# Hybrid decoder layer on eight cores: the first stages by token blocks, the first projection's 2048 columns resident, and the group map folded into the up projection

## What is computed

```python
hn = rmsnorm(x, g_mix)
z = hn @ w_in                      # 1024 -> 4096 columns: u | b | c | h (512 each) | gp | gc (1024 each)
# pooling branch: trailing windows 2/4/8/16 over four channel groups of 128
d = windowed_mean(u) - u
mixed = einsum('btgc,gcd->btgd', d, w_group) * scale
# conv branch: three taps, depthwise, causal
y = sum(w_conv[k] * shift(c * h, 2 - k) for k in range(3)); conv_out = b * y
merged = sigmoid(gp) * (mixed @ w_pool_up) + sigmoid(gc) * (conv_out @ w_conv_out)
x = x + merged @ w_o
# then a SwiGLU FFN (2816), and a gated per-layer embedding, with a final rmsnorm
```

## Time and profile before

| | |
|---|---|
| Runs | 1023.15 us median of 3 (1022.27 to 1025.79) |
| Profiled execution | 1024.13 us, of which the slowest core's span is 1022.5 us (cores 1016.4 to 1022.5) |
| PE busy | 964.5 us, 94% of the span |
| DVE, ACT, POOL busy | 483.6, 258.3, 319.6 us |
| Mean granted TensorE clock of that core | 0.976 |
| DMA | 63.18 MB written, mean 62 GB/s |

### The profile page before, as it was taken

The page is one execution under the profiler, slowest core; times in us unless marked ns, Lnnn a source line. Parts: engine busy times, 40 slices in busy tenths (PEclk is TensorE's granted clock), DMA queues, the critical chain, the costliest instruction groups (busy, mean ns, idle before and its releaser), DMA issues.

```text
span 1022.5 us, 15628 instructions; the slowest of 8 cores (1016.4 to 1022.5 us)
## 1 busy us (share of the span) xinstructions
PE 964.5 (94%) x5284; PEld 473.3 (46%) x5284; DVE 483.6 (47%) x606; ACT 258.3 (25%) x499; POOL 319.6 (31%) x314
## 2 busy tenths in 40 slices
PE   3679998899999999989999999999999999999995
PEld 3335444344454445544444444444444444455442
DVE  2563657522222228842824523622632362276887
ACT  2443332322222223321011111011011101155443
POOL 5346999443344430000001011001300420066422
PEclk8689999899999999999999999999999999999998
DMA  8754050763334466342326044224853510000433
GB/s 161 204 96 42 8 66 1 99 70 32 31 32 42 45 95 191 124 67 27 52 21 72 12 43 42 42 21 42 109 82 38 59 25 1 1 1 6 120 127 123
DMA packets 104220, 63.18 MB, mean 62 GB/s; under 512 B 89559, under 2 KB 91775, under 8 KB 104128
## 3 DMA queue, kind: packets, MB, share of 16 engines
q0 software_dynamic: 95728, 33.76, 30.1%
q1 hardware_dynamic: 7874, 27.60, 8.0%
q10 hardware_dynamic: 542, 0.84, 0.3%
HBM read 86.66 MB, written 9.50 MB: 94 GB/s over the span
## 4 chain that ended last, share of the span: by engine, by line
PE 85%; DVE 6%; DMA 3%; issue 2%; ACT 2%; POOL 0%; DVEq 0%; ACTq 0%; POOLq 0%; SPq 0%
PE psum L90 85%; DVE t L90 6%; DMA t<-xp 3%; ACT t L90 2%; POOL t L90 0%; DVEq L101 0%; DVEq L140 0%; ACTq L101 0%; POOLq L140 0%; ACT L90 0%; POOLq L101 0%; SPq L117 0%
## 5 line engine op out<-in xcount | busy, mean ns | idle before, releaser
L90 PE MATMUL psum<-t,t 128*128 128x512 bf16 (+2 forms) x5212 | 958.7, 347 | 47.4 <-DVE t L90 29.1
L90 PEld LDWEIGHTS psum<-t,t 128*128 128x128 bf16 (+1 forms) x5212 | 467.5, 99 | 538.2 <-issue 65.3
L90 DVE TENSOR_TENSOR t<-psum,t 128x1024 f32<-128x1024 f32 (+5 forms) x401 | 346.5, 869 | 459.0 <-PE psum L90 415.9
L90 ACT ACTIVATE t<-psum 128x128 f32<-128x128 f32 (+5 forms) x264 | 144.7, 551 | 588.2 <-PE psum L90 582.4
L90 POOL TENSOR_TENSOR t<-t,t 128x512 bf16<-128x512 f32 (+8 forms) x130 | 171.2, 1321 | 259.7 <-DVE t L90 226.4
L118 POOL DMA_DIRECT2D t<-w_ffn_in x44 | 38.9, 890 | 332.9 <-PE psum L90 332.6
L90 ACT ACTIVATE t<-t 128x1024 bf16<-128x1024 f32 (+3 forms) x128 | 84.5, 661 | 89.0 <-DVE t L90 59.9
L90 DVE SCALAR_TENSOR_TENSOR t<-t,t,t 128x512 f32<-128x512 f32 (+2 forms) x58 | 73.0, 1260 | 25.8 <-ACT t L90 17.3
L90 POOL TENSOR_TENSOR t<-t 128x2062 f32<-128x2062 f32 (+8 forms) x21 | 47.0, 2239 | 6.8 <-ACT t L90 4.2
L118 POOL DMA_DIRECT2D t<-w_in x32 | 28.8, 910 | 14.3 <-PE psum L90 13.3
L90 ACT ACTIVATE t<-t,t 128x512 f32<-128x512 f32 (+1 forms) x20 | 13.2, 658 | 65.6 <-DVE t L90 65.6
(11 more groups left out here) (14 smaller groups left out, 26.9 us busy)
## 6 DMA issues: line engine op xcount, KB each, us to landing
t<-xp SPq DMA_DIRECT2D x32, 512.0 KB, 4.5
t<-w_ffn_in POOLq DMA_DIRECT2D x44, 256.0 KB, 5.7
t<-w_in POOLq DMA_DIRECT2D x32, 256.0 KB, 7.5
yp<-t SPq DMA_DIRECT2D x16, 512.0 KB, 2.7
t<-w_ffn_out POOLq DMA_DIRECT2D x4, 1024.0 KB, 12.1
t<-w_o POOLq DMA_DIRECT2D x1, 2048.0 KB, 24.4
t<-w_ple_gate POOLq DMA_DIRECT2D x1, 2048.0 KB, 25.8
t<-w_ffn_out POOLq DMA_DIRECT2D x2, 768.0 KB, 9.4
```

Of the source, the lines that this page charges most:

```text
L90: fn = (lambda eng, meth=meth, kw=kw: getattr(eng, meth)(**kw))
```

## The change

- **Order.** Tokens are now outside and columns inside. Block 0 (512 tokens) takes all 16 column groups, then block 1, 2, 3; the 128 decode tokens are done inside the first chunk of stage 4, one column quadruple (u, c, h, b) after each of its first four token blocks.
- **Weights.** The 2048 columns of `w_in` that feed u, b, c, h stay resident in `wres` (4 MB in bf16). They come in five DMAs on POOL's queue, issued at the start: 256, 256, 512, 512, 512 columns wide, in the order u, u, c, h, b. They were 16 DMAs of 128 columns.
- **x tiles.** Five buffers instead of eight; tiles 0 and 1 are loaded at once, 2 and 3 behind 0 and 1, and tiles 4 and 5 only when the piece with the h columns has landed.
- **Normalisation.** The scaling is on DVE for tiles 0 to 3, on ACT from tile 4 on; none on POOL. The steps of the next block stand at fixed places between the column groups of the present one (table `NS`).
- **Windows.** POOL works on 527 elements at a time with the last level written to `wbuf`; mean and subtraction are one DVE instruction (`dop`), put off by three groups.
- **Group map.** `w_group` (transposed, times `scale`) is multiplied with `w_pool_up` once, four transposes and eight matmuls, into `wfuse`; `s2_gmm` and stage 4's loads of `w_pool_up` fall away. `pool_out` holds d itself.
- **Elsewhere.** The state rows go out after chunk 0 of stage 4, `w_o` is loaded after chunk 1 instead of before chunk 0, and chunk 0 has temporaries of its own.

```diff
--- before.py
+++ after.py
...
+    wres, o = sbt(o, [128, 8, 2048], BF16)
+    ubuf, o = sbt(o, [128, 4, 528], F32)
+    vbuf, o = sbt(o, [128, 4, 514], F32)
...
-        WL.append((wcol(w_pool_up, m_ * 128), 4))
...
+    WP = [(0, 256), (256, 512), (1024, 1536), (1536, 2048), (512, 1024)]
+
+    def wp_load(i):
+        a, b = WP[i]
+        em.dma("pool", wres[:, :, a:b], w_in[:, a:b].rearrange("(k p) n -> p k n", p=128), Dwp[i], writes=[Rwp[i]])
+
+    Rxin1 = [Res() for _ in range(NX1)]; Dxin1 = [em.newsem("dxin1%d" % i) for i in range(NX1)]
+    Rxn1 = [Res(), Res()]
+
+    def x_load(t, gate=()):
+        em.dma("sp", xin1[t % NX1][:, :], xtile(t), Dxin1[t % NX1], reads=list(gate), writes=[Rxin1[t % NX1]])
...
+    x_load(0)
+    x_load(1)
+    wp_load(0)
...
+    wp_load(1)
...
+    wp_load(2); wp_load(3); wp_load(4)
...
+    def n_b(t, eng):
+        rs, Rrs = nst[t]
+        xi = xin1[t % NX1]; xn_t = xn1[t % 2]
+        if eng == "dve":
+            em.op("dve", "tensor_scalar", dict(out=xn_t[:, :], in0=xi[:, :], scalar1=rs, scalar2=None, op0=ALU.mult),
+                  reads=[Rxin1[t % NX1], Rrs], writes=[Rxn1[t % 2]])
+        else:
+            em.op("act", "activation", dict(out=xn_t[:, :], in_=xi[:, :], func=AF.Copy, scale=rs),
+                  reads=[Rxin1[t % NX1], Rrs], writes=[Rxn1[t % 2]])
+
+    def n_c(t):
+        norm_back(xn1[t % 2], Rxn1[t % 2], 0, t)
+
+    def n_step(st, t, eng="act"):
+        if not 0 <= t < NT:
+            return
+        if st == "a":
+            nst[t] = n_a(t)
+        elif st == "b":
+            n_b(t, eng)
+            if t + NX1 < NT and t + NX1 >= 5:
+                x_load(t + NX1, [Rwp[3]] if t + NX1 < 6 else [])
+        else:
+            n_c(t)
+
...
+    def gmm(kind, cc, c0, n):
         b = nb()
...
+        col = UCOL[kind] + cc * 128
+        hres = [Rh[t] for t in range(c0 // 128, (c0 + n) // 128)]
+        for k in range(8):
+            em.op("pe", "matmul", dict(out=psum[:, b, 0:n], lhsT=wres[:, k, col:col + 128], rhs=hnT[:, k, c0:c0 + n],
+                                       start=(k == 0), stop=(k == 7)),
+                  reads=[wpres(kind, cc)] + hres, writes=[Rps[b]], sig=(k == 7))
+        return b
...
+    def dop(g, sb):
+        if sb == 4:
+            o_ = sj(pool_out[:, g, SEQ:NTOK]); w_ = sj(wbuf[:, g, 0:128]); u_ = us(g)[:, :, 15:23]
+        else:
+            o_ = pool_out[:, g, sb * 512:sb * 512 + 512]; w_ = wbuf[:, g, :]; u_ = ubuf[:, g, 15:527]
+        em.op("dve", "scalar_tensor_tensor", dict(out=o_, in0=w_, scalar=1.0 / wins[g], in1=u_, op0=ALU.mult, op1=ALU.subtract),
...
+        if last:
+            tree(g, sb)
+            later.append([6 if sb == 0 else 3, lambda: dop(g, sb)])
...
+    def g_h(cc, sb):
+        n = NB[sb]
+        b = gmm("h", cc, CB[sb], n)
...
+        em.op("dve", "tensor_tensor", dict(out=vo, in0=hi, in1=ci, op=ALU.mult), reads=[Rps[b], Rcs[cc]], writes=[Rv[cc]])
+        em.op("act", "activation", dict(out=ci, in_=v0, func=AF.Copy, scale=wconv[:, cc, 0:1]),
+              reads=[Rv[cc], Rwc], writes=[Rcs[cc]])
...
+        def taps():
+            em.op("dve", "scalar_tensor_tensor", dict(out=ci, in0=v1, scalar=wconv[:, cc, 1:2], in1=ci, op0=ALU.mult, op1=ALU.add),
+                  reads=[Rv[cc], Rwc], writes=[Rcs[cc]])
+            em.op("dve", "scalar_tensor_tensor", dict(out=ci, in0=v2, scalar=wconv[:, cc, 2:3], in1=ci, op0=ALU.mult, op1=ALU.add),
+                  reads=[Rv[cc], Rwc], writes=[Rcs[cc]])
+        later.append([1, taps])
...
+    x_load(2, [Rxin1[0]])
+    x_load(3, [Rxin1[1]])
+    x_load(4, [Rwp[3]])
...
+    def fuse_b(g):
+        for half in range(2):
             b = nb()
...
+            em.op("pe", "matmul", dict(out=psum[:, b, :], lhsT=wgT[:, g, :], rhs=wupb[:, g, half * 512:(half + 1) * 512], start=True, stop=True),
+                  reads=[Rwgt, Rwup], writes=[Rps[b]])
+            em.op("act", "activation", dict(out=wfuse[:, g, half * 512:(half + 1) * 512], in_=psum[:, b, :], func=AF.Copy),
+                  reads=[Rps[b]], writes=[Rwf[g]])
...
+    NS = [{9: [("a", 0)], 10: [("b", 0), ("a", 1)], 11: [("b", 1)], 12: [("c", 0), ("a", 2)], 13: [("b", 2), ("c", 1), ("a", 3)],
+           14: [("b", 3)], 15: [("c", 2), ("c", 3)]},
+          {0: [("a", 0)], 1: [("b", 0)], 3: [("a", 1)], 4: [("b", 1), ("c", 0)], 6: [("a", 2)], 7: [("b", 2), ("c", 1)],
+           9: [("a", 3)], 10: [("b", 3), ("c", 2)], 13: [("c", 3)]}]
+
+    def run_sb(sb):
+        if sb == 0:
+            order = [(k, c) for k in "chb" for c in range(4)]
+        else:
+            order = [(k, c) for c in range(4) for k in "uchb"]
+        for i, (k, c) in enumerate(order):
+            do(k, c, sb)
+            t = 4 * sb + 4
+            if sb < 4:
+                j = i + (4 if sb == 0 else 0)
+                for st, tt in NS[min(sb, 1)].get(j, []):
+                    n_step(st, t + tt)
...
+    def s3_between(tb):
+        if tb < 4:
+            for k_ in "uchb":
+                do(k_, tb, 4)
+        if tb == 3:
+            while later:
+                tick()
...
+            s4_chunk(0, s3_between)
+            s3_rows()
+            for m_ in range(1, 8):
+                for tb in range(5):
+                    Rm[m_][tb].inherit(*Rxin1, Rconst, Rust, Rvst, *Rs4[8:])
...
```

More of the change, by code:

```diff
@@ L301, in build_nc @@
     assert o <= C0 + 69632, o
+    o = C0 + 34816 + 8192
+    for i in range(6):
+        t_, o = sbt(o, [128, 512], F32)
+        s4buf.append(t_)
+    for i in range(2):
+        t_, o = sbt(XN_OFF + 2048 * i, [128, 512], F32)
+        s4buf.append(t_)
     o = C0 + 17408
@@ new lines, in n_c, with tick @@
+    def n_c(t):
[11 more added lines that the diff above has]
+            n_c(t)
+    def tick():
+        for d in list(later):
+            d[0] -= 1
+        for d in list(later):
+            if d[0] <= 0:
+                later.remove(d)
+                d[1]()
@@ new lines, in build_nc @@
+    n_step("a", 0)
+    n_step("b", 0, "dve")
+    consts()
+    n_step("a", 1)
+    n_step("b", 1, "dve")
+    n_step("c", 0); n_step("c", 1)
+    for g in range(2):
+        g_u(g, 0, 0, 256, False)
+    for t in (2, 3):
+        n_step("a", t)
+    for t in (2, 3):
+        n_step("b", t, "dve")
+    for g in range(2, 4):
+        g_u(g, 0, 0, 256, False)
+    for t in (2, 3):
+        n_step("c", t)
+    for g in range(4):
+        g_u(g, 0, 256, 256, True)
+        tick()
+    em.dma("act", wgf[:, :, :], w_pg.rearrange("g c d -> c g d"), Dmisc, writes=[Rwgf])
@@ new lines, in build_nc, with fuse_a @@
+    em.dma("pool", wupb[:, :, :], w_pool_up.rearrange("(g d) n -> d g n", d=128), Dwup, writes=[Rwup])
+    def fuse_a():
+        b = nb()
+        for g in range(4):
+            em.op("pe", "transpose", dict(out=psum[:, b, g * 128:(g + 1) * 128], in_=wgf[:, g, :], identity=identf[:, :]),
+                  reads=[Rwgf, Ridentf], writes=[Rps[b]], sig=(g == 3))
+        for g in range(4):
+            em.op("act", "activation", dict(out=wgT[:, g, :], in_=psum[:, b, g * 128:(g + 1) * 128], func=AF.Copy, scale=pscale[:, g:g + 1]),
+                  reads=[Rps[b], Rg0], writes=[Rwgt])
@@ new lines, in build_nc, with s3_rows @@
+    for sb in range(4):
+        run_sb(sb)
+    while later:
+        tick()
+    def s3_rows():
+        while later:
+            tick()
+        em.dma("sp", npp[:, :], ustage[113:128, 0, :], Dust, reads=[Rust], final=True)
+        for s in range(16):
+            em.dma("sp", nps[s, 7:15, :], ustage[s * 8:(s + 1) * 8, 1, :], Dust, reads=[Rust], final=True)
+        em.dma("sp", nps[:, 0:7, :], spool[:, 8:15, :], Dout, final=True)
+        em.dma("sp", ncp[:, :], vstage[126:128, 0, :], Dvst, reads=[Rvst], final=True)
+        for s in range(16):
+            em.dma("sp", ncs[s, :, :], vstage[s * 8 + 6:s * 8 + 8, 1, :], Dvst, reads=[Rvst], final=True)
```

539 lines of the change are left out of this document (215 added, 324 removed).

## The result

The changed kernel takes **1012.16 us** (median of 4, 1010.39 to 1012.79) beside 1023.15 for the one before on the same chip (median of its three fast runs; a fourth ran in the slower state, 1179.47 us, and no figure below uses such runs): ratio 0.9884 [0.9857, 0.9911], in brackets the 95% interval. A second set on another chip gave 1011.63 and 0.9856 [0.9841, 0.9871]. So it is faster, as forecast, but by 12 to 15 us (1.2 to 1.4%) where 28 were predicted, and outside the range of 984 to 1010. The profiled execution took 1012.55 us, its slowest core, 7, 1011.0.

What follows compares the result with a forecast made beforehand. PE was taken as the bound, with 59 us lost ahead of stage 4. The terms summed to 167.4 us at stage 4's start against 194.6; with 0.5 more, 27.7 less gave 996.4 profiled, 995.5 forecast, range 984 to 1010.

Steps and rivals of the forecast that it cites:

- What bounds the kernel before: Ahead of stage 4, which began at 194.6 us, PE had 135.5 us of work, so 59 us were lost there.
- Item 1: Start and weight arrival: T0, the end of block 0, at 55 us, with weights and x written at 190 GB/s.
- b's wait of 7 us: In block 0, PE done with h at 38 us was to wait for b's piece, taken to land at 45.
- tile 7's chain: At the end of block 0, the chain of x tile 7, without distance in `NS`, was booked at some 1.3 us.
- rule on round-robin: DMA engines alternate between queues packet by packet; b would land at 48, T0 58, the total 3 us above the forecast.
- Rival B: Weights late at the start: x holds them off or 1 KB rows run at 130 GB/s; T0 67 to 70, 1009; chance 0.14.
- Rival C: All smoother: b lands at 38, T0 47, waits of 3 instead of 9; 982 to 988 us; chance 0.13.
- Item 2: Blocks 1 to 3: PE at 29 us a block, the other engines keeping up, 3 us booked for boundaries.
- Rival D: DVE becomes the bound at 35.5 us a block, 24 us more in all: about 1019; chance 0.07 with milder forms.
- Item 3: Decode tokens in chunk 0 of stage 4: 7.0 us of PE work moved there and 5.5 us of new waits.
- Item 4: State rows after chunk 0 delay chunk 1's first merge to about 20 us into it, costing PE 0.5 us.
- The last half microsecond: Half a microsecond more gain, for what the clock regains with fewer pauses.

Runs made afterwards that it cites:

- b1: The kernel before with its group map and the scale left out, in the old order; 1024.52 us, 0.9981 of the kernel before.
- e3: The changed kernel with the same resident weight columns loaded in 16 pieces of 128 columns; 1017.70 us, 0.9924 of the kernel before.
- e5: The changed kernel with the resident weights loaded in three pieces of 512, 1024 and 512 columns; 1015.50 us, 0.9902 of the kernel before.
- e1: The changed kernel with the c, h and b pieces held back until the second u piece has landed; 1016.37 us, 0.9901 of the kernel before.
- e4: The changed kernel with block 0's taps one group later, its last window's subtraction three later, norms of tiles 4 to 7 one earlier; 1009.49 us, 0.9841.
- e9: The changed kernel with block 0's eight taps on DVE left out (part of the computation missing); ratio 0.983 to the kernel before.
- e13: e4 plus decode conv-state transposes one group later, x tiles 4 and 5 let out at the c piece's landing, norms one more place earlier; 0.9819.

## Why the prediction was right and wrong

**What bounds the kernel before: right.** 59 us lost ahead of stage 4; the change gets 13.65 of them back at the sigmoid, and its gain lies there alone. The fusion is at most a small part of it (b1).

**Item 1, T0 = 55: wrong, the step that failed.** It has two halves. "Rows of 1 KB as here are in no row; they lie between 175 and 192 ... I take 190" was the first: the weights came at 146 GB/s (133 by the queue's share), and c starts 15 us late. e3 and e5 show that packet width has a part in it, and e1 that the later pieces in flight cost the latest core 3 to 5 us; that the rows behind the 190 were taken while the neighbouring core hardly wrote is seen in the traces, but no run tested what it does. The second is b's wait of 7 us. The size of that stretch came out right by chance (31.7 us for 31) and the cause was another: the conv branch's and the norms' steps in code order on DVE and ACT (e4, e9), with the transfer close beneath (e13). The text dealt with tile 7's chain alone, as 1.3 us, and put the norms of tiles 4 to 6 at nothing. The rule on round-robin of the Trainium skill (DMA: Bandwidth & Descriptors, Queues, rings and completion order) put b at 48 and so nearer its 51.1; but since on this core nobody waited for it, T0 tells nothing for or against the rule. The trace has 0.09 MB on the weights' queue beside 2.34 MB of x between 44 and 52 us: nearly all of b had been written before the x tiles met it.

**Rival B** named what came: "rows of 1 KB run at 130 GB/s", T0 67 to 70, 1009. It had 0.14, held off by the argument that few x tiles are let out ahead of h, which says nothing on the weights' own rate. Even so it was right only in the first half of the miss. Rival C's argument, w_o's 192 GB/s, rested on a window of 4 us with mostly narrow packets. The range ended at 1010, inside B, and so just short of the result.

**Item 2, blocks 1 to 3: right in the main,** and better than booked. Chunk 0 starts at 162.6 (ACT's table load, which waits for the chunk's first eight matmuls, ends its wait at 164.36), 91.8 us after T0, and not one wait of PE is seen; the 3 us booked for boundaries did not come. PEclk is 0.57 in 71 to 75 us, behind the waits at the end of block 0 (the first two groups of block 1 take 2.9 and 2.3 us in place of 1.74), and 1.00 from 75 to 162 us, so the clock did fall, for a moment, where the prediction had named that as a sign of being wrong. DVE is busy 50.37 of 90 us. Rival D is out.

**Item 3, decode tokens: right.** The waits are 0.87, 0.91, 0.88, 0.91, 1.61 and 0.45, 5.6 us for 5.5 booked. Chunk 0 takes 40.5 us, over the 35 that I had set as a mark of being wrong; the mark was set without the float32 transposes, 22 of which run in chunk 0 and which item 2's 6 us had booked. From T0 to the sigmoid the plan had 141.5 us and it took 139.3.

**Item 4, state rows: right.** nps has 8.37 us of issue, ncs 5.92, and POOL's first merge of chunk 1 comes 11.7 us into it (214.80 less 210.06 - 32 x 0.217), ahead of the 20 expected; PE doesn't wait:

```profile
214.80 2.49 POOL L90 TENSOR_TENSOR t<-t,t 128x512 bf16<-128x512 f32 x2 [9.46 <-DMA ncs<-t]
```

**The last half microsecond: wrong in sign.** From the sigmoid to the end it takes 800.9 us, before 798.8. The 2.1 us are not at an instruction: at the same place of the program, 425 to 440 us after and 438.54 to 453.54 before, the windows show the same work at another clock:

```profile
425.00:440.00 15.00, 13.54 (x64) 6.38 (x63) 6.74 (x9) 3.07 (x4) 0.00 (x0) 0.89 0.31 53
```

```profile
438.54:453.54 15.00, 13.54 (x72) 6.36 (x70) 6.86 (x9) 3.63 (x6) 0.00 (x0) 1.00 0.41 81
```

As recorded, that is eight matmuls fewer in as long a stretch. The fall is no property of the changed kernel alone: from the sigmoid to the end all its eight cores take 800.8 to 801.4 us, while six cores of the kernel before take 798.7 to 799.2 and cores 1 and 3 take 801.0 and 801.7, with PEclk at 0.66 in 435 to 440 and 0.75 in 440 to 445 us. Why the clock fell on some and not on others is open. Together: 15.8 late, 2.2 regained up to the sigmoid, 2.1 and 0.5 lost behind it, 16.2 in all, which is 1012.55 less the 996.4 predicted for the profiled execution.

## What to carry to other kernels

Price a transfer by its own queue and from a stretch like the one to come: the same packet width, the same kind of load (with a cast or without), tens of microseconds long, and with the neighbouring core as busy as it will be; a GB/s of a mixed or short window belongs to none of these. MB over share times stretch keeps two queues apart, but it is no ceiling where the share exceeds 100%. Where a stage starts by filling a resident buffer, the slowest core's last piece sets the time, so read all cores before trusting one; the scatter between them is also an experiment that costs nothing. An edit that changes the order of the groups also moves whatever is placed by counting them, and a gate on a load empties the queue for a while: check both before reading such a run. And where engines take work in code order, a steady state that keeps up says nothing of the first block, in which everything that waited for the data comes at once: count there what stands ahead of each norm step.

## What was unexpected in the hardware

- Cast loads cost a DMA engine 47 ns of its share for 252 bytes written, 114 for 953 and 183 for 1610; by the clock, with all cores loading, that was 113, 146 and 151 GB/s. Plain loads of x had 316 GB/s by the share, and in 44 to 48 us, when nearly all that moves is x, core 7 writes 383 GB/s.
- Packets of 256 B moved at 175 GB/s in 90 to 93 us of the kernel before, with the neighbouring core nearly idle, and at 113 in e3 with all cores loading.
- Neighbouring cores are served unevenly: in every pair of both runs of the changed kernel, one gets its second piece 2.6 to 7.0 us ahead of the other. Which one isn't fixed: in the pair 6/7 it changed between the two.
- Two of DVE's additions of 16 columns take 1.12 us at 45.67 us, beside POOL's window additions, and 0.45 us at 50.02 us, when POOL has done.
